# A decoder layer on one core: attention output at the next step's front, operands made in the preceding loops, ScalarE's and VectorE's heads written out

## The chip, the cores and the metric

The kernel runs on one core of one Trainium2 chip. The metric is the device time of one execution, in microseconds (us). Short names of the engines: PE is TensorE (matmuls), ACT is ScalarE, DVE is VectorE, POOL is GpSimd, SP is SyncE, which here issues nearly all transfers. SBUF holds operands, PSUM the products of PE.

## The reference

One inference step of one decoder layer over 520 columns: 512 prompt tokens and 8 sequences with one new token each (`D_MODEL` 2048, `D_FF` 5632, all f32).

```
h = rms_norm(x, norm_mix)
z = h @ w_in                       # q_a k_a v_a | q_r f_r i_r g_r, 8 + 8 heads of 128
...
o_att = rms_norm(o_att, att_gain) * (1.0 - lam_init)
...
o_rnn = rms_norm(o_rnn.astype(x.dtype), rnn_gain) * jax.nn.silu(g_r...)
x = x + jnp.concatenate([o_att, o_rnn], axis=-1) @ w_out
ffn, conv_buf = conv_ffn(rms_norm(x, norm_ffn), conv_buf0, w_gate, w_up, conv_w, conv_b, w_down)
x = x + ffn
x = x + jax.nn.sigmoid(rms_norm(x, norm_ple) @ w_ple_gate) * (p @ w_ple_proj)
```

`o_att` is differential attention (two softmaxes, the second subtracted with a weight), `o_rnn` a gated linear recurrence with a state. `conv_ffn` is silu(causal conv of 3 over h W_gate) times (h W_up), times W_down. Keys, values and states are outputs too.

## The kernel before

**Weights.** Every weight matrix comes in chunks of 8 tiles of 128x128 (6 and 5 in W_down). SP's `load` fetches a chunk into one of two raw buffers. ACT's `split` rounds it to `w_hi`, DVE's `low` makes the remainder `w_lo`. PE's `passes` then run five matmuls for each tile (lines 914 to 918) over the 520 columns of the activation, which is held in two parts too (`act_hi` and `act_lo`, both called act in the rows). A `split` waits until PE has used the chunk two before it (`w_used`). Products alternate between two PSUM banks, G[0] and G[1]. DVE empties a bank with `scaled` (lines 1467 to 1471) or `added` (lines 1475 and 1477, into the residual xT), which frees it for PE (`product_free`).

**Small products.** Everything else on PE is a small task in one of two scratch banks, M[0] and M[1], in turn. A task waits until the reader of the task two before it has set `free` of that bank.

**Heads.** There are 9 steps. Step h multiplies the 14 chunks of head h in the order q, k, v, f, i, r, g (28 slots of 4 tiles), with the attention of head h and the recurrence of head h − 1 as small tasks behind the slots that the tables `ATTENTION` and `RECURRENCE` name. The last step has only the recurrence and takes chunks of W_out. q uses bank 0, and so does g. PE's steps are written out; on ACT, DVE and SP the seven steps from 1 to 7 are a loop (`Fori`). At the front of a step PE runs a tiny product (`pad`, which ends the step before) and `ssq_a`, the sum of squares of the attention output; `att_out`, the attention output itself (weights wT times v_nat, 20 matmuls, line 797), stands behind slot 25 of its own step. From `ssq_a` ACT and DVE make the normalised output mix_a, which goes to memory; SP waits for it (`mix_a_done`) ahead of its loads of the key pages.

**Between the stages.** The next product's operands are made by ACT (`operand`, a copy scaled by the norm's gain) and DVE (the remainder, line 1712), k = 0 to 15, after the loop of the preceding stage, at both boundaries: W_out to ConvFFN, and ConvFFN to the last stage (PLE). Before the first ConvFFN product PE also sums the squares of x (`ss_out`, line 716), and ACT's `norm` makes the factor R from it: a table load, Ln, a table load, Exp. ConvFFN has 4 groups of 11 blocks; in the first block of each, PE runs `c_old` (line 1008) behind two chunks, a turn of old convolution rows that 11 transfers (`conv_in`) bring.

Of the kernel before, what the change touches and what calls it, by code (L numbers as in the profile page):

```python
# [65 lines left out]
KC = 8  # L66
# [34 lines left out]
}  # L101
RECURRENCE = {
    0: ["ssq_a"], 3: ["i_nat"], 7: ["kh_nat"], 9: ["upd"], 11: ["intra"], 14: ["rnn"], 16: ["s_upd"], 18: ["s_rnn"], 19: ["s_rnn_turn"], 20: ["ssq_r"],
# [72 lines left out]
EARLY_MIXED = 3  # L176
# [53 lines left out]
def program(nc, a, o):  # L230
# [56 lines left out]
    wT = hb("wT", [P, 10, P])  # L287
    k_pages = hb("k_pages", [P, NPG, P])
    k_nat = hb("k_nat", [P, 5, P])
    v_nat = hb("v_nat", [P, 5, P])  # L290
# [189 lines left out]
    def _(sp):  # L480
# [62 lines left out]
        def step(plan, it, h, r, pages):  # L543
            attention = any("ssq_q" in x for x in plan)
            recurrence = any("ssq_r" in x for x in plan)
            for s in range(HALVES):
                if attention and (not isinstance(h, int) or s >= 2 * EARLY_CHUNKS):
                    weights(h, s)
                if not attention and s % 2 == 0:
# [37 lines left out]
        def visit(what, arg):  # L587
# [4 lines left out]
            elif what == "heads":  # L592
# [3 lines left out]
                elif h1 == HEADS:  # L596
# [11 lines left out]
                    b, v = scratch.task("att_out", HEADS - 2)  # L608
# [4 lines left out]
                    for k in range(HEADS // 2, KT):  # L613
                        if k not in MIX_DIRECT:
                            mix_back(k)
                    for k in MIX_DIRECT:
                        x_back(k)
# [19 lines left out]
            elif what == "ffn":  # L637
                with sp.Fori(0, GROUPS) as g:
# [19 lines left out]
                    with sp.Fori(0, KT // 2) as m:  # L658
                        for j in range(4):
                            k0, n = ((0, 6), (6, 5))[j % 2]  # L660
                            load(g * GROUP_CHUNKS + m * 4 + (C_FFN + FF_CHUNKS + j), j % 2, w_down, g * GF + k0, n, m * (2 * P) + (j // 2) * P)
            elif what == "ple":
# [17 lines left out]
    def _(pe):  # L680
# [38 lines left out]
        def small(name, it, h, r):  # L719
# [73 lines left out]
            elif name == "att_out":  # L793
                b = task(name, it, [], (), ["w2", "w3", "v_nat"])
# [4 lines left out]
            elif name == "ssq_a":  # L799
                wide(name, it, [("sq_a", n)], K("ones"), sq)  # L800
# [53 lines left out]
        def step(plan, it, h, r):  # L854
            if r is not None:
                small("ssq_a", it, r, None)
            for s in range(HALVES):
# [25 lines left out]
                for name in plan[s]:  # L883
                    if name != "ssq_a":
                        small(name, it, h, r)
            pad(it)
# [34 lines left out]
        def full_product(g, n_free, c, sizes, x, wait_k=None, slot0=0, k0=0, wait_last=None):  # L921
# [3 lines left out]
            for j, n in enumerate(sizes):  # L925
# [6 lines left out]
                k += n  # L932

        sum_task = None

        def visit(what, arg):
# [33 lines left out]
            elif what == "out":  # L970
# [24 lines left out]
                wide("ss_out", 0, [("sq_sum_done", SUM_EARLY + KT)], K("ones"), sq_sum)  # L995
                pad(0)
            elif what == "ffn":
                with pe.Fori(0, GROUPS) as g:
                    def ff_block(f, first):
                        n = g * GF + f  # L1000
                        for x in range(2):
                            full_product(x, g * g_per_group + f + g_ffn[x], g * GROUP_CHUNKS + f * 4 + (C_FFN + 2 * x), (KC, KC), act2,
                                         ("act_lo_ready", 2 * KT + 1) if first and x == 0 else None)
# [14 lines left out]
                    with pe.Fori(0, KT // 2) as m:  # L1018
                        pe.wait_ge(flag("u_done"), g * GF + (GF - 1))
                        for x in range(2):  # L1020
                            full_product(x, g * g_per_group + m + (g_ffn[x] + GF), g * GROUP_CHUNKS + m * 4 + (C_FFN + FF_CHUNKS + 2 * x), DOWN_TILES, u2,
                                         wait_last=("u_done", g * GF + GF))
            elif what == "mid":
# [49 lines left out]
    def _(act):  # L1073
# [18 lines left out]
        def small(name, it, h, r):  # L1092
            n = None if h is None else h + 1
            m = None if r is None else r + 1
            if name in ("ssq_q", "ssq_k", "ssq_r"):
# [8 lines left out]
                elif name == "ssq_q":  # L1104
                    if h is not None and not isinstance(h, int):
# [10 lines left out]
            elif name in ("k_nat", "v_nat"):  # L1116
                dst, outs = (k_nat, ("k_prompt", "k_sample")) if name == "k_nat" else (v_nat, ("v_prompt", "v_sample"))
                b = take(name, it)
                if not isinstance(h, int):
# [35 lines left out]
            elif name == "att_out":  # L1155
# [3 lines left out]
                sb_, sv = scratch.task("s_turn", it)  # L1159
                act.wait_ge(free[sb_], sv)  # L1160
# [35 lines left out]
        def step(plan, it, h, r):  # L1196
            for s in range(HALVES):
# [22 lines left out]
                if r is not None and s == 0:  # L1220

# [8 lines left out]
                    func(r_e[:, :], r_k[:, 0:SEQ], ACT.Ln, bias=K("tiny")).then_inc(flag("log_k"), 1)  # L1230
                    b = take("ssq_a", it)
# [19 lines left out]
                for name in plan[s]:  # L1251
                    if name != "ssq_a":
# [15 lines left out]
        def operand(k, src, gain):  # L1268

            func(act_hi[:, k, :], src, ACT.Copy, scale=gain).then_inc(flag("act_hi_ready"), 1)  # L1270
# [22 lines left out]
        def visit(what, arg):  # L1293
# [30 lines left out]
            elif what == "heads":  # L1324
# [3 lines left out]
                elif h1 == HEADS:  # L1328
                    with act.Fori(h0, h1) as h:
# [3 lines left out]
            elif what == "out":  # L1333
# [17 lines left out]
                func(pT_hi[:, :, :], pT[:, :, :], ACT.Copy).then_inc(flag("pT_hi_done"), 1)  # L1351
                with act.Fori(KT // 4, KT // 2) as it:
                    for x in range(2):
                        out_product(it, x)
                for k in range(KT):
# [4 lines left out]
                    operand(k, xT[:, k, :], vec(ROWS_A["norm_ffn"] + k))  # L1360
                norm(*scratch.task("ss_out", 0))
            elif what == "ffn":
                with act.Fori(0, GROUPS) as g:
                    def ff_block(f, first):
# [7 lines left out]
                        if first:  # L1372
                            b = take("c_old", g)
# [18 lines left out]
                    with act.Fori(0, KT // 2) as m:  # L1392
                        for x in range(2):
# [3 lines left out]
                            squares(g * KT + m * 2 + (SUM_EARLY + KT + x), x, column(xT, m * 2 + x))  # L1397
            elif what == "mid":
                for k in range(KT):
                    act.wait_ge(w_used, C_PLE)  # L1400
                    if k >= KT - 2:
                        act.wait_ge(g_free[k % 2], g_ple[k % 2])
                    operand(k, xT[:, k, :], vec(ROWS_A["norm_ple"] + k))
# [46 lines left out]
    def _(dve):  # L1450
# [34 lines left out]
        def small(name, it, h, r):  # L1485
# [34 lines left out]
            elif name.startswith("score"):  # L1520
# [4 lines left out]
                if i > 0 or not isinstance(h, int):  # L1525
# [95 lines left out]
        def step(plan, it, h, r):  # L1621
            for s in range(HALVES):
# [60 lines left out]
                if r is not None and s == 6:  # L1683
                    dve.wait_ge(flag("exp_b"), r + 1)
                    dve.wait_ge(flag("r_qm_done"), r + 1)
                    dve.tensor_tensor(r_qd, z_r[:, 0:SEQ], r_e[:, :], ALU.mult).then_inc(flag("r_qd_done"), 1)
                if h is not None and s in ROTATE_AT:
# [4 lines left out]
            pad(it)  # L1692
# [16 lines left out]
        def operand(k, src, gain, n):  # L1709

            dve.wait_ge(flag("act_hi_ready"), n)
            dve.scalar_tensor_tensor(act_lo[:, k, :], src, gain, act_hi[:, k, :].bitcast(F32), ALU.mult, ALU.subtract).then_inc(flag("act_lo_ready"), 1)  # L1712
# [17 lines left out]
        def visit(what, arg):  # L1730
# [54 lines left out]
            elif what == "heads":  # L1785
# [3 lines left out]
                elif h1 == HEADS:  # L1789
                    with dve.Fori(h0, h1) as h:  # L1790
# [3 lines left out]
            elif what == "out":  # L1794
# [17 lines left out]
                with dve.Fori(KT // 4, KT // 2) as it:  # L1812
                    for x in range(2):
                        out_product(it, x)
                pad(0)
                for k in range(KT):
                    operand(k, xT[:, k, :], vec(ROWS_A["norm_ffn"] + k), 2 * KT + k + 1)
                dve.wait_ge(flag("R_ready"), 2)
            elif what == "ffn":
# [3 lines left out]
                with dve.Fori(0, GROUPS) as g:  # L1823
                    with dve.Fori(0, GF) as f:
# [14 lines left out]
                        dve.wait_ge(full[b], v - 1)  # L1839
                        scaled(0, ffg[:, 2:T + 2], g * g_per_group + f + (g_ffn[0] + 1))  # L1840
# [20 lines left out]
                        dve.tensor_tensor(column(u_lo, f), ffu[:, :], column(u_hi, f).bitcast(F32), ALU.subtract).then_inc(flag("u_done"), 1)  # L1861
                    dve.memset(sq_sum[:, :], 0.0).then_inc(flag("sum_zeroed"), 1)
                    with dve.Fori(0, KT // 2) as m:
                        for x in range(2):
# [7 lines left out]
                            add_squares(g * KT + m * 2 + (SUM_EARLY + KT + x), x)  # L1872
            elif what == "mid":
                pad(0)
                for k in range(KT):
                    operand(k, xT[:, k, :], vec(ROWS_A["norm_ple"] + k), 3 * KT + k + 1)
# [100 lines left out]
```

## Time and profile before

| | before |
|---|---|
| time, median of 3 runs | 2856.32 us (2855.97 to 2856.54) |
| the profiled execution's own time | 2855.82 us |
| its span in the profile | 2854.0 us |
| PE busy | 2807.3 us (98%) |
| DVE busy | 1514.7 us (53%) |
| ACT busy | 1042.5 us (37%) |
| mean granted clock of PE | 0.993 |

PE, a matmul pipeline whose ends are modelled, is hardly ever idle over the whole span. A granted clock of 1.00 is the higher of its two levels (2.4 GHz), 0.50 the lower (1.2 GHz).

### The profile page before, as it was taken

To read this page: it belongs to the slowest core of one execution; us is meant where nothing else is said; L and a number is where in the kernel's file an instruction comes from. 1 tells how busy PE (TensorE), PEld (TensorE's weight loads), DVE (VectorE), ACT (ScalarE), POOL (GpSimd) and SP (SyncE) were. 2 spreads that over 40 slices of the span, in tenths; PEclk is the share of its full clock that TensorE was granted. 3 is DMA by queue.
4 is the path that set the end of the run, shared out by engine and by line. 5 is a ranking of instruction groups with operands and counts; after the bars stand their busy time and mean duration, and the time that the engine had idled before them with its cause. 6 is when DMAs were issued, how large, how long until landed. Compare 5 with 4: busy or idle time off the path is not lost.

```text
span 2854.0 us, 53939 instructions
## 1 busy us (share of the span) xinstructions
PE 2807.3 (98%) x20395; PEld 2583.9 (91%) x20395; DVE 1514.7 (53%) x2547; ACT 1042.5 (37%) x1457; POOL 20.1 (1%) x19
## 2 busy tenths in 40 slices
PE   6999999999999999999999999999999999999998
PEld 6888888888888998999999999999999999998998
DVE  5565565565566545445544445544455444455444
ACT  4455455455455234222332223322223322234322
POOL 2000000000000000000000000000000000000000
PEclk8999999999999999999999999999999999999999
DMA  5343343343345332332333332333323333332332
GB/s 195 99 124 105 101 123 109 96 124 111 97 125 189 111 89 82 88 95 82 92 100 88 90 94 84 93 97 88 91 84 94 97 91 88 89 88 85 106 110 83
DMA packets 547886, 291.20 MB, mean 102 GB/s; under 512 B 15848, under 2 KB 538914, under 8 KB 547786
## 3 DMA queue, kind: packets, MB, share of 16 engines
q1 hardware_dynamic: 516762, 268.49, 32.4%
q10 hardware_dynamic: 31040, 21.46, 2.4%
q8 instruction: 69, 1.13, 0.2%
q14 instruction: 15, 0.12, 0.0%
HBM read 268.44 MB, written 21.63 MB: 102 GB/s over the span
## 4 chain that ended last, share of the span: by engine, by line
PE 93%; DVE 4%; ACT 1%; issue 1%; ACTq 0%; SPq 0%; DVEq 0%; DMA 0%
PE product L914 28%; PE product L918 15%; PE product L916 15%; PE product L915 14%; PE product L917 14%; PE scratch L708 2%; PE scratch L716 1%; DVE w_lo L1454 1%; DVE act L1712 1%; PE scratch L797 1%; PE scratch L758 1%; DVE s_state L1607 1%; ACT w_hi L1079 1%; ACT score L1090 0%; PE scratch L813 0%
## 5 line engine op out<-in xcount | busy, mean ns | idle before, releaser
L914 PE MATMUL product<-act,w_hi 128*128 128x512 f32 x2816 | 1142.3, 406 | 21.1 <-DVE act L1712 14.2
L1454 DVE TENSOR_TENSOR w_lo<-w_raw,w_hi 128x1024 fp32r<-128x1024 f32 (+1 forms) x496 | 594.4, 1198 | 562.2 <-ACT w_hi L1079 561.9
L1079 ACT ACTIVATE w_hi<-w_raw 128x1024 fp32r<-128x1024 f32 (+1 forms) x496 | 514.7, 1038 | 975.7 <-PE product L918 941.2
L918 PE MATMUL product<-act,w_lo 128*128 128x264 f32 x2816 | 806.4, 286 | 0.0
L916 PE MATMUL product<-act,w_hi 128*128 128x264 f32 x2816 | 802.2, 285 | 0.0
L915 PE MATMUL product<-act,w_hi 128*128 128x264 f32 x2816 | 800.6, 284 | 0.0
L917 PE MATMUL product<-act,w_lo 128*128 128x256 f32 x2816 | 793.2, 282 | 0.0
L916 PEld LDWEIGHTS product<-act,w_hi 128*128 128x128 f32 x2816 | 531.3, 189 | 128.2
L914 PEld LDWEIGHTS product<-act,w_hi 128*128 128x128 f32 x2816 | 534.3, 190 | 46.7 <-issue 38.9
L915 PEld LDWEIGHTS product<-act,w_hi 128*128 128x128 f32 x2816 | 533.9, 190 | 0.8
L918 PEld LDWEIGHTS product<-act,w_lo 128*128 128x128 f32 x2816 | 533.4, 189 | 0.0
L917 PEld LDWEIGHTS product<-act,w_lo 128*128 128x128 f32 x2816 | 531.1, 189 | 0.0
L914 PE MATMUL product<-u,w_hi 128*128 128x512 f32 x704 | 278.5, 396 | 0.0
L1467 DVE TENSOR_TENSOR low_part<-product,R 128x256 f32<-128x256 f32 x160 | 67.6, 423 | 292.0 <-PE product L918 289.3
L916 PE MATMUL product<-u,w_hi 128*128 128x264 f32 x704 | 200.1, 284 | 0.0
L915 PE MATMUL product<-u,w_hi 128*128 128x264 f32 x704 | 199.3, 283 | 0.0
L918 PE MATMUL product<-u,w_lo 128*128 128x264 f32 x704 | 198.8, 282 | 0.0
L917 PE MATMUL product<-u,w_lo 128*128 128x256 f32 x704 | 197.0, 280 | 0.0
L916 PEld LDWEIGHTS product<-u,w_hi 128*128 128x128 f32 x704 | 132.1, 188 | 31.5
L1475 DVE TENSOR_TENSOR xT<-product,xT 128x520 f32 (+1 forms) x96 | 67.1, 699 | 160.2 <-PE product L918 160.2
L914 PEld LDWEIGHTS product<-u,w_hi 128*128 128x128 f32 x704 | 132.1, 188 | 0.8 <-DVE w_lo L1454 0.7
L918 PEld LDWEIGHTS product<-u,w_lo 128*128 128x128 f32 x704 | 132.7, 188 | 0.0
(251 smaller groups left out, 2266.4 us busy)
## 6 DMA issues: line engine op xcount, KB each, us to landing
w_raw<-in_w_in SPq DMA_DIRECT2D x112, 512.0 KB, 3.8
w_raw<-in_w_gate SPq DMA_DIRECT2D x88, 512.0 KB, 3.8
w_raw<-in_w_up SPq DMA_DIRECT2D x88, 512.0 KB, 3.8
w_raw<-in_w_down SPq DMA_DIRECT2D x64, 384.0 KB, 3.3
w_raw<-in_w_down SPq DMA_DIRECT2D x64, 320.0 KB, 3.1
w_raw<-in_w_out SPq DMA_DIRECT2D x32, 512.0 KB, 4.1
w_raw<-in_w_ple_gate SPq DMA_DIRECT2D x32, 384.0 KB, 3.3
k_pages<-in_cache_k SPq DMA_DIRECT2D x128, 64.0 KB, 2.5
```

Source lines behind the costliest of these rows:

```text
L708: return pe.transpose(out, in_, ident[0:n, 0:n])
L716: mm = pe.matmul(M[b][:, half, 0:TH], lhsT, rhs[:, half * TH:(half + 1) * TH], start=True, stop=True)
L758: mm = pe.matmul(M[b][:, m_, 0:w], q_rot[rows, i * P:(i + 1) * P], k_rot[rows, 0:w], start=True, stop=True)
L914: pe.matmul(both, hi, x[:, k, :, 0:TA], start=begin, stop=False)
L915: pe.matmul(far, hi, x[:, k, 1, TA:T], start=begin, stop=False)
L916: pe.matmul(far, hi, x[:, k, 0, TA:T], start=False, stop=False)
L917: pe.matmul(near, lo, x[:, k, 1, 0:TA], start=False, stop=end)
L918: mm = pe.matmul(far, lo, x[:, k, 1, TA:T], start=False, stop=end)
L1079: act.activation(w_hi[:, slot, 0:n, :], w_raw[:, slot, 0:n, :], ACT.Copy).then_inc(w_hi_ready, 1)
L1454: dve.tensor_tensor(flat(w_lo[:, slot, 0:n, :]), flat(w_raw[:, slot, 0:n, :]), flat(w_hi[:, slot, 0:n, :]).bitcast(F32), ALU.subtract).the ...
L1467: dve.tensor_tensor(low_part[:, :], low_sums(G[g]), R[:, 0:TA], ALU.mult).then_inc(g_low[g], 1)
L1475: dve.tensor_tensor(x, high_sums(G[g]), x, ALU.add).then_inc(g_low[g], 1)
```

## The change

- `att_out` moves from behind slot 25 of its step to the front of the next, and `ssq_a` from the front to behind slot 1. `pad` moves from the end of a step to behind slot 26. On ACT the copy of `att_out` and the Square that feeds `ssq_a` move with it, and so does the read of `ssq_a`. In the last step SP fetches most parts of the mixed output after `s_turn`, a task before `att_out`, and the rest after `att_out`; four, not three, of DVE's early mixes come first.
- ACT's and DVE's loops over the heads become written-out code.
- The ConvFFN operands 0 to 7 are made inside the second half of the W_out loop, 8 to 15 after it. `ss_out` runs behind the first ConvFFN chunk, and ACT's `norm` behind the splits of two chunks.
- All PLE operands are made inside the down loop of the last group. For that, group 0 on every engine and the last group on ACT and DVE are written apart.
- SP issues a group's 11 `conv_in` transfers ahead of its first two chunks, not behind them.

```diff
-    21: ["score3"], 22: ["w2"], 24: ["w3", "s_out"], 25: ["s_turn", "att_out"],
+    21: ["score3"], 22: ["w2"], 24: ["w3", "s_out"], 25: ["s_turn"],
...
-    0: ["ssq_a"], 3: ["i_nat"], 7: ["kh_nat"], ...
+    0: ["att_out"], 1: ["ssq_a"], 3: ["i_nat"], 7: ["kh_nat"], ...
...
-EARLY_MIXED = 3
+EARLY_MIXED = 4
+PAD_AT = 26
...
             if r is not None:
-                small("ssq_a", it, r, None)
+                small("att_out", it, r, None)
...
-            pad(it)
+                if s == PAD_AT:
+                    pad(it)
...
-                wide("ss_out", 0, [("sq_sum_done", SUM_EARLY + KT)], K("ones"), sq_sum)
+                sum_task = scratch.task("ss_out", 0)
...
+                def sum_out():
+                    sum_of_squares(SUM_EARLY + KT)
...
+                                         after=sum_out if isinstance(g, int) and first and x == 0 else None)
...
                 if r is not None and s == 0:
+                    small("att_out", it, r, None)
...
+                if r is not None and s == 1:
                     b = take("ssq_a", it)
...
-                    with act.Fori(h0, h1) as h:
+                    for h in range(h0, h1):
                         step(plan, h - 1, h, h - 1)
...
+                act.wait_ge(w_used, C_RNN)
                 with act.Fori(KT // 4, KT // 2) as it:
                     for x in range(2):
                         out_product(it, x)
-                for k in range(KT):
+                        operand_of("norm_ffn", it * 2 + (x - KC))
+                for k in range(KC, KT):
...
-                norm(*scratch.task("ss_out", 0))
+                norm_task = scratch.task("ss_out", 0)
...
                         two_chunks(0)
                         if first:
+                            if isinstance(g, int) and g == 0:
+                                norm(*norm_task)
                             b = take("c_old", g)
...
+                            if final:
+                                operand_of("norm_ple", m * 2 + x)
...
-                    with dve.Fori(h0, h1) as h:
+                    for h in range(h0, h1):
...
-                    ffn_chunk(0, 0)
-                    ffn_chunk(0, 1)
-
-                    sp.wait_ge(full[0], scratch.task("c_old", g)[1] - 1)
-
-                    sp.wait_ge(flag("conv_out"), g * 32 + 16)
+                    if isinstance(g, int):
+                        sp.wait_ge(flag("pT_lo_done"), 1)
+                    else:
+                        sp.wait_ge(full[0], scratch.task("c_old", g)[1] - 1)
...
                         sp.dma_start(conv_in[j:j + 2 * NS, i // 2, :], ...).then_inc(flag("conv_in"), 16)
+                    ffn_chunk(0, 0)
+                    ffn_chunk(0, 1)
```

How PE's order changes between the first two steps. Before, behind the last tile of the g product (its last matmul is the first row):

```order
L918 MATMUL product<-act,w_lo 128x264
L852 MATMUL scratch<-const 32x64 [waits scratch1_free]
L716 MATMUL scratch<-sqx,const 128x260 [waits sq_a,scratch0_free]
L716 MATMUL scratch<-sqx,const 128x260
L914 MATMUL product<-act,w_hi 128x512 [waits product0_free,w_lo_ready]
```

And of the change, the same place, and behind the eight tiles of slots 0 and 1 (the program lines of `passes` are now 926 to 930):

```order
L930 MATMUL product<-act,w_lo 128x264
L808 MATMUL scratch<-wT,v_nat 128x128 [waits scratch0_free]
L808 MATMUL scratch<-wT,v_nat 128x128 x9
L926 MATMUL product<-act,w_hi 128x512 [waits product0_free,w_lo_ready]
...
L930 MATMUL product<-act,w_lo 128x264
L727 MATMUL scratch<-sqx,const 128x260 [waits sq_a,scratch1_free]
L727 MATMUL scratch<-sqx,const 128x260
L926 MATMUL product<-act,w_hi 128x512 [waits w_lo_ready]
```

Ten products (`att_out`; the profile counts each as two matmuls) stand where the pad and `ssq_a` stood, and `ssq_a` has moved eight tiles on.

How ACT's order changes between W_out and ConvFFN. Before, with act an operand, R the norm's factor, product0 and product1 the two product banks:

```order
L1090 ACTIVATE act<-xT,vecs 128x520 [waits w_used] x14
L1090 ACTIVATE act<-xT,vecs 128x520 [waits product0_free,w_used]
L1090 ACTIVATE act<-xT,vecs 128x520 [waits product1_free,w_used]
L1090 ACT_TABLE_LOAD
L1090 ACTIVATE R<-scratch,const 128x520 [waits scratch0_full]
L1090 ACT_TABLE_LOAD
L1090 ACTIVATE R<-R 128x520 [waits scratch0_free]
...
L1079 ACTIVATE w_hi<-w_raw 128x1024 [waits w_used]
...
L1090 ACTIVATE conv_old<-scratch 128x2x6x16 [waits scratch0_full]
```

And of the change:

```order
L1112 ACTIVATE act<-xT,vecs 128x520 [waits w_used] x6
L1112 ACTIVATE act<-xT,vecs 128x520 [waits product0_free,w_used]
L1112 ACTIVATE act<-xT,vecs 128x520 [waits product1_free,w_used]
L1101 ACTIVATE w_hi<-w_raw 128x1024 [waits w_used,w_landed0]
L1101 ACTIVATE w_hi<-w_raw 128x1024 [waits w_used,w_landed1]
L1112 ACT_TABLE_LOAD
L1112 ACTIVATE R<-scratch,const 128x520 [waits scratch0_full]
L1112 ACT_TABLE_LOAD
L1112 ACTIVATE R<-R 128x520 [waits scratch0_free]
L1112 ACTIVATE conv_old<-scratch 128x2x6x16 [waits scratch0_full]
```

Eight operands are gone from here, and the two splits now stand ahead of the two operations on R. On PE the tasks of that place, before `c_old` and after it in the change (line 1026), read:

```order
L727 MATMUL scratch<-sq_sum,const 128x260 [waits sq_sum_done,scratch0_free]
L727 MATMUL scratch<-sq_sum,const 128x260
L926 MATMUL product<-act,w_hi 128x512 [waits act_lo_ready,w_lo_ready]
...
L1026 MATMUL scratch<-const,conv_in 128x16 [waits conv_in,scratch0_free]
L1026 MATMUL scratch<-const,conv_in 128x16 x10
L926 MATMUL product<-act,w_hi 128x512 [waits w_lo_ready,product1_free]
```

`ss_out` now stands between the first and the second chunk, and `c_old`, behind the second, uses the same scratch bank.

## Rows read from the trace of the kernel before

**Rows 1.** The page, busy time, share of the span and instructions of PE:

```profile
PE 2807.3 (98%) x20395; PEld 2583.9 (91%) x20395; DVE 1514.7 (53%) x2547; ACT 1042.5 (37%) x1457; POOL 20.1 (1%) x19
```

**Rows 2.** Waits of PE: total us, times, longest us.

```profile
PE product L914 <- DVE act L1712: 14.2, 8, 4.3
...
PE product L914 <- DVE z_g L1468: 6.8, 8, 2.2
...
PE scratch L843 <- DVE s_ro L1613: 1.4, 7, 0.2
```

**Rows 3.** Timeline of PE around a step's front: start us, us, instruction, [idle before].

```profile
244.52 2.48 PE L797 MATMUL scratch<-wT,v_nat 128*128 128x128 f32 x20
...
252.89 1.14 PE L716 MATMUL scratch<-sqx,const 128*128 128x260 f32 x4
254.79 0.47 PE L914 MATMUL product<-act,w_hi 128*128 128x512 f32 x1 [0.76 <-DVE z_g L1468]
...
255.59 0.40 PE L914 MATMUL product<-act,w_hi 128*128 128x512 f32 x1
...
276.11 1.04 PE L716 MATMUL scratch<-sqx,tables 128*128 128x260 f32 x4
...
277.69 0.39 PE L914 MATMUL product<-act,w_hi 128*128 128x512 f32 x1
...
278.41 0.40 PE L914 MATMUL product<-act,w_hi 128*128 128x512 f32 x1
...
280.21 0.47 PE L914 MATMUL product<-act,w_hi 128*128 128x512 f32 x1
```

**Rows 4.** Timeline of PE, front of the last step:

```profile
894.58 0.47 PE L914 MATMUL product<-act,w_hi 128*128 128x512 f32 x1 [2.18 <-DVE z_g L1468]
```

**Rows 5.** Timeline of DVE around the same step's front:

```profile
253.61 0.42 DVE L1467 TENSOR_TENSOR low_part<-product,R 128x256 f32<-128x256 f32 x1 [0.47 <-issue]
...
275.02 1.23 DVE L1454 TENSOR_TENSOR w_lo<-w_raw,w_hi 128x1024 fp32r<-128x1024 f32 x1 [3.79 <-ACT w_hi L1079]
```

**Rows 6.** Timeline of ACT around the same step's front:

```profile
247.04 0.60 ACT L1090 ACTIVATE oT<-scratch 128x512 f32<-128x512 f32 x1 [2.16 <-PE scratch L797]
...
253.84 1.28 ACT L1090 ACT_TABLE_LOAD   x1
...
273.93 1.06 ACT L1079 ACTIVATE w_hi<-w_raw 128x1024 fp32r<-128x1024 f32 x1 [2.07 <-DMA w_raw<-in_w_in]
```

**Rows 7.** Timeline of PE, W_out to ConvFFN:

```profile
1092.18 2.07 PE L716 MATMUL scratch<-sq_sum,const 128*128 128x260 f32 x4 [3.29 <-DVE sq_sum L1719]
...
1108.70 1.51 PE L1008 MATMUL scratch<-const,conv_in 16*128 16x16 f32 x22
```

**Rows 8.** Timeline of ACT there:

```profile
1102.36 0.70 ACT L1090 ACTIVATE R<-scratch,const 128x520 f32<-128x520 f32 x1
```

**Rows 9.** Windows: length, busy PE, PEld, DVE, ACT, POOL; granted clock, DMA share, GB/s.

```profile
892.00:898.00 6.00, 3.82 (x26) 3.23 (x24) 5.90 (x12) 5.59 (x7) 0.00 (x0) 1.00 1.06 368
1092.00:1098.80 6.80, 5.62 (x18) 4.30 (x19) 4.19 (x9) 6.80 (x12) 0.00 (x0) 0.50 0.04 10
2626.00:2634.00 8.00, 7.26 (x37) 6.74 (x38) 8.00 (x13) 8.00 (x14) 0.00 (x0) 0.79 0.17 49
```

**Rows 10.** Timeline of PE, ConvFFN to PLE:

```profile
2626.74 0.47 PE L914 MATMUL product<-act,w_hi 128*128 128x512 f32 x1 [3.70 <-DVE act L1712]
```

**Rows 11.** Timeline of SP's queue, group 0 to 1; the page's DMA issues (KB, us to landing).

```profile
1457.94 8.15 SPq L495 DMA_DIRECT2D w_raw<-in_w_down  x3
1469.88 4.04 SPq L495 DMA_DIRECT2D w_raw<-in_w_gate  x2
1474.17 5.55 SPq L652 DMA_DIRECT2D conv_in<-in_state_ffn_conv  x11
...
w_raw<-in_w_gate SPq DMA_DIRECT2D x88, 512.0 KB, 3.8
```

**Rows 12.** Timeline of ACT, group 0 to 1:

```profile
1475.16 1.06 ACT L1079 ACTIVATE w_hi<-w_raw 128x1024 fp32r<-128x1024 f32 x1 [2.07 <-PE product L918]
```

More of the change, by code:

```diff
@@ L548, in step @@
                     weights(h, s)
+                if not attention and s == 0:
+                    b, v = scratch.task("att_out", it)
+                    sp.wait_ge(full[b], v)
+                    for k in range(MIX_DIRECT[0] + 1, MIX_DIRECT[1]):
+                        mix_back(k)
+                    x_back(MIX_DIRECT[1])
                 if not attention and s % 2 == 0:
@@ L607, in visit @@
                         mix_back(k)
-                    b, v = scratch.task("att_out", HEADS - 2)
+                    b, v = scratch.task("s_turn", HEADS - 2)
                     sp.wait_ge(full[b], v)
@@ L612, in visit @@
                     sp.wait_ge(flag("v_nat_out"), HEADS * 32)
[L613 to L617, printed above, removed]
+                    for k in range(HEADS // 2, MIX_DIRECT[0]):
+                        mix_back(k)
+                    x_back(MIX_DIRECT[0])
                 else:
@@ L637, in visit, with group @@
             elif what == "ffn":
-                with sp.Fori(0, GROUPS) as g:
+                def group(g):
                     def ffn_chunk(f, j):
@@ L661, in visit @@
                             load(g * GROUP_CHUNKS + m * 4 + (C_FFN + FF_CHUNKS + j), j % 2, w_down, g * GF + k0, n, m * (2 * P) + (j // 2) * P)
+                group(0)
+                with sp.Fori(1, GROUPS) as g:
+                    group(g)
             elif what == "ple":
@@ L932, in full_product @@
                 k += n
+                if after is not None and j == 0:
+                    after()
         sum_task = None
@@ L1022, in visit @@
                                          wait_last=("u_done", g * GF + GF))
+                group(0)
+                with pe.Fori(1, GROUPS) as g:
+                    group(g)
             elif what == "mid":
@@ L1158, in small @@
                 act.wait_ge(free[b], scratch.task(name, it)[1])
-                sb_, sv = scratch.task("s_turn", it)
-                act.wait_ge(free[sb_], sv)
+                sb_, sv = scratch.task("ssq_a", it)
+                act.wait_ge(free[sb_], sv - 1)
                 func(sq[:, :], oT[:, :], ACT.Square).then_inc(flag("sq_a"), 1)
@@ L1251, in step @@
                 for name in plan[s]:
-                    if name != "ssq_a":
+                    if name not in ("ssq_a", "att_out"):
                         small(name, it, h, r)
@@ L1397, in visit @@
                             squares(g * KT + m * 2 + (SUM_EARLY + KT + x), x, column(xT, m * 2 + x))
-            elif what == "mid":
[L1399 to L1403, printed above, removed]
+                            if final:
+                                operand_of("norm_ple", m * 2 + x)
+                group(0)
+                with act.Fori(1, GROUPS - 1) as g:
+                    group(g)
+                group(GROUPS - 1, final=True)
+            elif what == "mid":
                 norm_task = scratch.task("ss_ffn", 0)
@@ L1691, in step @@
                         small(name, it, h, r)
-            pad(it)
             if r is not None and h is not None:
@@ L1872, in visit @@
                             add_squares(g * KT + m * 2 + (SUM_EARLY + KT + x), x)
+                            if final:
+                                operand_of("norm_ple", m * 2 + x, m * 2 + (3 * KT + x + 1))
+                ff_block(0, 0)
+                with dve.Fori(1, GF) as f:
+                    ff_block(0, f)
+                down(0)
+                with dve.Fori(1, GROUPS - 1) as g:
+                    with dve.Fori(0, GF) as f:
+                        ff_block(g, f)
+                    down(g)
+                with dve.Fori(0, GF) as f:
+                    ff_block(GROUPS - 1, f)
+                down(GROUPS - 1, final=True)
             elif what == "mid":
                 pad(0)
-                for k in range(KT):
-                    operand(k, xT[:, k, :], vec(ROWS_A["norm_ple"] + k), 3 * KT + k + 1)
             elif what == "ple":
```

48 lines of the change are left out of this document (28 added, 20 removed).

## The prediction

> **What bounds the kernel now.** I read the page first: TensorE (PE) is busy 98% of a span of 2854.0 us, so only what PE waits for, and what a slow clock costs it, can be won [rows 1]. Next the waits of PE. Three entries belong to places that the change touches: 14.2 us for act (the operands of a matrix product), 6.8 us in 8 pieces for z_g and 1.4 us for s_ro [rows 2]. Of act's only what the timeline shows at the two stage boundaries below can be won; the setup and the last stage are left alone. Then I opened the timeline at each place to see what a wait costs with its restart.
>
> **Front of a head's step (att_out and ssq_a).** The last product of a step lies in bank 0, and the first of the next step needs that bank. Between them PE has a tiny pad and ssq_a, and then waits for VectorE's z_g. From ssq_a's start to the second tile pass 255.59 − 252.89 = 2.70 us; the same four matmuls in mid-stream take 277.69 − 276.11 = 1.58 us [rows 3]. The boundary costs 1.12 us, of which 0.76 is printed as idle; 0.36 is restart. Eight boundaries: 6.8 + 8 × 0.36 = 9.7 us.
> The change puts att_out there instead. Its 20 matmuls take 2.48 us to their last end [rows 3], and they need nothing of the step's last product. VectorE needs 254.79 − 253.61 = 1.18 us from low_part's start to z_g's release, and began 0.47 us late behind "issue", the loop's back-edge [rows 3, 5]; even 0.47 + 1.18 = 1.65 us fits under 2.48. ssq_a then runs between two slots, where it costs its mid-stream price, 1.58 − 0.72 = 0.86 us (a tile is 278.41 − 277.69 = 0.72) [rows 3]; it loses nothing but its place. The work itself is the same. At the last boundary VectorE does early mixes ahead of z_g and PE idles 2.18 us [rows 4]; now four of them, but with the pad's wait gone they can begin before the step's last product ends, so I leave 0.3 us. Term: **9.4 us** (6.0 if the restarts stay and 0.8 us is left at the last boundary; 9.7 at most).
>
> *What becomes late.* ScalarE's copy of att_out (0.60 us) and a Square as long stood far ahead of the boundary, at 247.04; now they stand behind att_out. That would start near 252.7 and end near 255.2, so copy and Square last to 256.4 and the table load that was at 253.84 follows then: **2.5 us later** [rows 3, 6]. Behind it queue the gates of the recurrence, the rsqrt of ssq_a, and by it mix_a; SP holds k_pages, and with them weight loads, until mix_a is done. The split at 273.93 shows this: it waited 2.07 us for its weights. Its w_lo is done at 275.02 + 1.23 = 276.25 and PE comes to that chunk at 280.21: 3.96 us of slack [rows 3, 5, 6]. 2.5 us of it go, nothing is paid. This is cover that a slower transfer would use up (rival C).
>
> **Heads of ScalarE and VectorE without loops.** One row shows a loop's price: "issue" 0.47 us ahead of low_part, already counted above [rows 5]. Elsewhere the only tight wait is s_ro, 1.4 us in seven steps [rows 2]; constants in place of registers may shorten its chain by some of that. No row says how much: 0 to 1.4, and I take the middle, **0.7 us**.
> The Trainium skill, "Runtime: NRT & Kernel Launch" (Instruction fetch mechanics), says that fetch is sequential and mostly hidden, and that a taken branch out of the fetched window stalls. The 0.47 us, once in each turn of the loop, agrees with the second half; by that alone the loops would give back at most 6 × 0.47 = 2.8 us, and here those lie under att_out in any case. No row shows the first half for VectorE.
>
> **Output projection to ConvFFN.** Before: PE's last tile ends at 1092.18 − 3.29 = 1088.89, it waits 3.29 us for sq_sum, runs the sum of squares at half clock, waits again for act, and reaches c_old at 1108.70, two weight chunks later [rows 2, 7]. After: operands 0 to 7 were made in the loop, so the first chunk starts near 1089.05 behind the pad; 8 tiles × 0.72 bring 1094.8; the sum of squares 0.86 brings 1095.65; the second chunk ends at 1101.4. Operands 8 to 15 begin as soon as the loop ends, and the whole first chunk, 5.75 us, lies ahead of the tile that needs the first of them.
> Here a **new wait** comes. c_old and ss_out share scratch bank 0, so c_old must wait until ScalarE's Ln has read the sum. The change puts that Ln behind the split of the chunk after next, which may begin only when PE has finished the chunk just before c_old. So from 1101.4: split 1.06, table load 1.28, Ln 0.70 and some 0.2 us of hand-overs, 3.2 us [rows 6, 8]. c_old starts at about 1104.7: 4.0 us earlier than before, not the 7.2 us that the chunks had won.
> PE idles 3.2 us there, and what followed such pauses differs: after 3.29 us the granted clock was 0.50 for 6.8 us; after 2.18 us it stayed 1.00; after 3.70 us it was 0.79 over 8 us [rows 4, 7, 9, 10]. That is a loss of 0, of 8 × 0.21 = 1.7, or of up to half of 5.62 busy us, 2.8. I take 1.7. Term: **2.3 us** (1.2 to 4.0).
>
> **ConvFFN to PLE.** All 16 operands now come out of the last down loop. PE waited 3.70 us for them and then ran 8 us at a clock of 0.79: 3.70 + 1.7 = **5.4 us** [rows 9, 10]; at least 3.7, if a wait for a scratch bank stops the clock from staying up. The scratch bank of the sum of squares is not needed again until a chunk later; ScalarE's Ln, no longer behind 16 operands, is in time.
>
> **conv_in ahead of a group's first chunks.** SP's 11 issues take 5.55 us and now stand before w_gate's two. SP is free from 1457.94 + 8.15 = 1466.1, so w_gate goes out near 1472.0, not at 1469.88; it lands 3.8 us later (the median of its 88), at 1475.8. The split took it at 1475.16, having waited for PE, so it comes 0.7 us later; split, w_lo and hand-over (1.06 + 1.23 + 0.2) bring 1478.3, and PE needs it 5 tiles after 1475.1, at 1478.7 [rows 11, 12]. Hidden by 0.4 us. With the spread of landings I charge **0.4 us** for three boundaries; 3 us if each is 1 us late.
>
> **Sum.** 9.4 + 0.7 + 2.3 + 5.4 − 0.4 = 17.4 us. The profiled execution took 2855.82 us itself, 0.5 under the median of 2856.32; from the median the forecast is 2838.9, so **2839 us**. Bounds: least 6.0 + 0 + 1.2 + 3.7 − 3 = 7.9 (2848.4), most 9.7 + 1.4 + 4.0 + 5.4 = 20.5 (2835.8).
>
> **Rivals.**
> A. *No stop at c_old.* If the Ln reads its sum before that split, both chunks' gain stays: 7.2 and no clock loss instead of 2.3, so 2834. Against it speaks the program order on ScalarE, which puts both splits first; for it only that a hand-over could be missing from my reading.
> B. *The heads' wait moves.* If z_g is late from another cause (the mixes, or a low_part that queues behind a late w_lo), the heads give only the back-edges, 2.8 us, instead of 10.1: 17.4 − 7.3 = 10.1, so 2846. VectorE is busy half of the time, and z_g has 0.8 us to spare under att_out; little speaks for this.
> C. *Slower: the heads' weights come late.* ScalarE's chain is 2.5 us later in each of seven steps, and SP's page loads and weight loads with it. It costs nothing up to 3.96 us. If queueing on SP doubles the delay to 5.0, PE waits 1.0 us a step; that makes 7 us and still a gain. Slower than now it would be from 17.4 / 7 = 2.5 us a step on, a delay of 6.5 us; at 7 us, 3.0 × 7 = 21, so 2860. The rows show only 2.07 us of waiting for a transfer there, so I give it little.
> D. *Nothing to measure.* Were C's delay some 5.5 to 7 us, or the written-out code slow to arrive by as much, gain and loss would cancel: 2852 to 2860. PE's heads are written out already, and PE waits for nothing but other engines.
>
> **Chances.** My forecast, all terms within their bounds, 0.74 (2835 to 2844); A 0.10; B 0.09; C 0.04; D 0.03. The range 2834 to 2846 takes in A and B's edge. Some 0.2% (5.7 us) is what a measurement here can tell from no change: faster 0.92, within 0.2% 0.04, slower 0.04.
>
> **What would show it.** In the profile after, z_g should be gone from PE's waits, and the step of a head be some 1.1 us shorter. A wait of PE's c_old line for ScalarE's R of about 3.2 us, with a granted clock under 1 behind it, would show the new stop; if it is absent, A holds. At the start of PLE no wait for act and a full clock. At the three group boundaries no wait for w_lo. A wait of PE for w_lo in mid-step, or for z_g still, would prove the head term wrong.

## The result, and the profile after

The changed kernel takes 2840.29 us (median of 6 runs, 2838.44 to 2841.87), the kernel before 2856.14 us beside it (6 runs, 2855.35 to 2856.69): 15.85 us less, a ratio of 0.9944 with a 95% interval of 0.9931 to 0.9957. The profiled execution took 2838.44 us, the shortest of the six; its span is 2836.7 us.

The page, as [rows 1], and waits of PE, as [rows 2] (total us, times, longest us):

```profile
PE 2799.5 (99%) x20395; PEld 2580.4 (91%) x20395; DVE 1516.2 (53%) x2547; ACT 1034.1 (36%) x1450; POOL 20.0 (1%) x19
```

```profile
PE product L926 <- DVE act L1747: 9.6, 7, 4.3
...
PE scratch L727 <- DVE sq_sum L1758: 3.3, 1, 3.3
PE scratch L1026 <- ACT R L1112: 3.2, 1, 3.2
...
PE scratch L727 <- ACT sqx L1112: 1.0, 1, 1.0
PE product L926 <- DVE w_lo L1488: 0.7, 2, 0.4
...
PE scratch L854 <- DVE s_ro L1647: 0.2, 1, 0.2
```

z_g (6.8 us before) is gone, and act has fallen from 14.2 to 9.6 us. What is left of act, the 3.3 us for sq_sum and the 1.0 us for sqx lie in the setup. The fall of s_ro from 1.4 to 0.2 looks larger than it is: the list leaves out waits below 0.15 us, and in PE's timeline each of the seven has only shrunk from some 0.19 to 0.14 us. Two entries behind the setup are new: c_old (line 1026) waits 3.2 us for R, and PE twice for w_lo.

Both kernels run the same 3520 weight tiles in the same order, so the starts of the same tile in both timelines say where time was won. The last column is the change of the difference since the row above.

| a tile just behind | before, us | after, us | difference | won here |
|---|---|---|---|---|
| the setup | 72.21 | 70.75 | 1.46 | 1.46 |
| front of step 1 | 154.90 | 152.43 | 2.47 | 1.01 |
| front of step 2 | 261.32 | 257.72 | 3.60 | 1.13 |
| front of step 7 | 793.26 | 784.18 | 9.08 | 5.48 |
| front of the last step | 901.11 | 889.49 | 11.62 | 2.54 |
| the last step's small tasks | 980.91 | 969.60 | 11.31 | −0.31 |
| c_old of group 0, and the slow clock behind it | 1112.40 | 1098.74 | 13.66 | 2.35 |
| start of group 1 | 1479.27 | 1465.82 | 13.45 | −0.21 |
| start of group 2 | 1859.91 | 1847.04 | 12.87 | −0.58 |
| start of group 3 | 2241.27 | 2229.01 | 12.26 | −0.61 |
| start of PLE (its sixth tile) | 2631.94 | 2614.55 | 17.39 | 5.13 |

The −0.31 us in the last step is the pad, which now stands behind slot 26 there.

The 1.46 us in the setup are not the change's: up to that tile PE, ACT and DVE run the same instructions in both. The clock differed. From 60 to 68 us the granted clock was 0.57 before and 1.00 after (windows as [rows 9], before and after):

```profile
60.00:68.00 8.00, 5.90 (x20) 5.25 (x21) 3.33 (x15) 4.71 (x8) 0.47 (x2) 0.57 0.45 125
```

```profile
60.00:68.00 8.00, 5.83 (x38) 5.43 (x39) 4.18 (x20) 4.78 (x8) 0.47 (x2) 1.00 0.42 119
```

Five of the seven other profiled executions below that have the changed kernel's setup reach the same tile 0.8 to 1.4 us later, with a granted clock of 0.57 to 0.79 there; the other two have 1.00 and reach it at the same time. Without the setup 15.9 us are left, which is what the medians differ by.

A step's front after, as [rows 3]; PE's timeline, start us, us, instruction:

```profile
248.17 2.39 PE L808 MATMUL scratch<-wT,v_nat 128*128 128x128 f32 x20
250.32 0.48 PE L926 MATMUL product<-act,w_hi 128*128 128x512 f32 x1
...
256.14 1.04 PE L727 MATMUL scratch<-sqx,const 128*128 128x260 f32 x4
256.82 0.58 PE L926 MATMUL product<-act,w_hi 128*128 128x512 f32 x1
...
276.63 0.47 PE L926 MATMUL product<-act,w_hi 128*128 128x512 f32 x1
```

att_out runs 2.39 us and the first tile follows with no idle time printed. On DVE and ACT, as [rows 5, 6]:

```profile
248.47 0.43 DVE L1501 TENSOR_TENSOR low_part<-product,R 128x256 f32<-128x256 f32 x1 [3.02 <-PE product L930]
248.81 0.69 DVE L1502 TENSOR_TENSOR z_g<-product,R 128x520 f32<-128x520 f32 x1
...
272.26 1.23 DVE L1488 TENSOR_TENSOR w_lo<-w_raw,w_hi 128x1024 fp32r<-128x1024 f32 x1 [4.61 <-ACT w_hi L1101]
```

```profile
250.60 0.60 ACT L1112 ACTIVATE oT<-scratch 128x512 f32<-128x512 f32 x1 [1.09 <-PE scratch L808]
251.23 0.64 ACT L1112 ACTIVATE sqx<-oT 128x520 f32<-128x520 f32 x1
251.89 1.28 ACT L1112 ACT_TABLE_LOAD   x1
...
271.17 1.06 ACT L1101 ACTIVATE w_hi<-w_raw 128x1024 fp32r<-128x1024 f32 x1 [2.88 <-DMA w_raw<-in_w_in]
```

z_g is ready at 249.5, 0.8 us before PE asks for its bank at 250.32. ACT's table load comes 251.89 − 248.17 = 3.72 us after the step's front; before, 253.84 stood 0.95 us behind ssq_a's start at 252.89, with the pad ahead of that. Counted from the end of the step's last product, the chain is thus about 2.5 us later, as worked out ahead. PE itself comes 0.9 us later to the chunks behind slot 1, since ssq_a now runs ahead of them. Against PE's tiles, which are 3.60 us earlier here, the table load is therefore only 1.65 us later (253.84 − 3.60 = 250.24, now 251.89), the page loads in SP's queue 1.3 us (266.17 − 3.60 = 262.57, now 263.86), and the weight split behind them 0.8 us (273.93 − 3.60 = 270.33, now 271.17). Its w_lo is done at 273.49, 3.1 us before PE's tile at 276.63.

That is one chunk. Two chunks earlier, the cover from the end of w_lo to PE's tile went from 4.3 us to 3.0, before and after:

```profile
261.89 1.23 DVE L1454 TENSOR_TENSOR w_lo<-w_raw,w_hi 128x1024 fp32r<-128x1024 f32 x1 [0.26 <-ACT w_hi L1079]
...
267.40 0.50 PE L914 MATMUL product<-act,w_hi 128*128 128x512 f32 x1
```

```profile
259.58 1.22 DVE L1488 TENSOR_TENSOR w_lo<-w_raw,w_hi 128x1024 fp32r<-128x1024 f32 x1
...
263.81 0.50 PE L926 MATMUL product<-act,w_hi 128*128 128x512 f32 x1
```

Of the chunks that lost cover, one in the last step has the least left. At that step's third chunk it went from 1.4 us (w_lo done at 905.80, the tile at 907.21) to 0.4:

```profile
893.93 1.22 DVE L1488 TENSOR_TENSOR w_lo<-w_raw,w_hi 128x1024 fp32r<-128x1024 f32 x1
...
895.58 0.50 PE L926 MATMUL product<-act,w_hi 128*128 128x512 f32 x1
```

W_out to ConvFFN, PE as [rows 7], and ACT as [rows 8]:

```profile
1083.55 1.04 PE L727 MATMUL scratch<-sq_sum,const 128*128 128x260 f32 x4
...
1093.53 1.51 PE L1026 MATMUL scratch<-const,conv_in 16*128 16x16 f32 x22 [3.21 <-ACT R L1112]
1094.97 0.79 PE L926 MATMUL product<-act,w_hi 128*128 128x512 f32 x1
...
1096.43 0.63 PE L926 MATMUL product<-act,w_hi 128*128 128x512 f32 x1
```

```profile
1090.42 1.06 ACT L1101 ACTIVATE w_hi<-w_raw 128x1024 fp32r<-128x1024 f32 x1 [4.08 <-PE product L930]
1091.49 1.28 ACT L1112 ACT_TABLE_LOAD   x1
1092.79 0.69 ACT L1112 ACTIVATE R<-scratch,const 128x520 f32<-128x520 f32 x1
```

The split ends ACT's wait when PE ends the chunk; table load and Ln follow, and c_old starts 0.05 us after Ln. The tiles behind it stand 1.46, 1.30 and 1.01 us apart instead of 0.72; from 1095.0 to 1098.4 the granted clock was 0.50.

At PLE's start there is no wait, tiles follow at 0.72 us from the first, and the granted clock of the 8 us is 1.00 [rows 9, 10]:

```profile
2610.00:2618.00 8.00, 8.00 (x54) 7.20 (x54) 4.64 (x7) 4.77 (x6) 0.00 (x0) 1.00 0.34 100
```

At a group's start ACT now waits for w_gate, at the same places as [rows 11, 12] (SP's queue at groups 1 and 2, ACT at group 1, PE at groups 2 and 3):

```profile
1452.93 5.36 SPq L656 DMA_DIRECT2D conv_in<-in_state_ffn_conv  x11
1458.54 1.78 SPq L497 DMA_DIRECT2D w_raw<-in_w_gate  x2
...
1840.54 1.36 SPq L497 DMA_DIRECT2D w_raw<-in_w_gate  x2
```

```profile
1462.62 1.06 ACT L1101 ACTIVATE w_hi<-w_raw 128x1024 fp32r<-128x1024 f32 x1 [3.21 <-DMA w_raw<-in_w_gate]
```

```profile
1847.04 0.50 PE L926 MATMUL product<-act,w_hi 128*128 128x512 f32 x1 [0.38 <-DVE w_lo L1488]
...
2229.01 0.50 PE L926 MATMUL product<-act,w_hi 128*128 128x512 f32 x1 [0.34 <-DVE w_lo L1488]
```

### The profile page after: what moved, and what is told of

The parts are those of the page before. It is cut to its first block, busy times and chain, and to the rows that moved or that the text cites. A ratio compares the mean times of both kernels' runs of the same rounds, so it can differ in the third digit from the quotient of the medians.

```text
span 2836.7 us, 53314 instructions
## 1 busy us (share of the span) xinstructions
PE 2799.5 (99%) x20395; PEld 2580.4 (91%) x20395; DVE 1516.2 (53%) x2547; ACT 1034.1 (36%) x1450; POOL 20.0 (1%) x19
## 4 chain that ended last, share of the span: by engine, by line
PE 93%; DVE 3%; ACT 2%; issue 1%; SPq 1%; DMA 0%; ACTq 0%; DVEq 0%
PE product L926 28%; PE product L930 14%; PE product L928 14%; PE product L927 14%; PE product L929 14%; PE scratch L719 2%; PE scratch L727 1%; DVE w_lo L1488 1%; ACT w_hi L1101 1%; ACT score L1112 1%; PE scratch L808 1%; DVE act L1747 1%; PE scratch L769 1%; DVE s_state L1641 1%; PE scratch L824 0%
```

## The experiments

Theory: att_out covers z_g at the steps' fronts whatever the loops cost; both stage boundaries win by operands made earlier; c_old's new wait comes from Ln's place behind a split; conv_in's place costs a little. The rivals are named in each expectation. The first four kernels shared their runs of the kernel before (median 2857.03 us), the last four too (2856.67 us).

**Is it the moved att_out or the written-out code?** The changed kernel with loops again:

```diff
-                    for h in range(h0, h1):
+                    with act.Fori(h0, h1) as h:
...
-                    for h in range(h0, h1):
+                    with dve.Fori(h0, h1) as h:
```

> The changed kernel with the heads of ScalarE and VectorE in loops again, all else as changed. Theory 1 (att_out at the front covers z_g whatever the loop costs): the back-edge of 0.47 us and the 1.18 us to z_g fit under att_out, PE has no wait for z_g at the steps' fronts, only the waits for s_ro come back: 0.9 to 1.4 us more than the changed kernel, some 2841.5 us. Theory 2 (the loop's back-edge was the wait, and the written-out code won the heads' time): PE waits for z_g again in six steps, 0.47 to 0.76 us each with 0.36 us of restart: 5 to 7 us more, some 2846 us.

Measured: 2841.12 us, 0.9944 of before (0.9931 to 0.9958). PE's waits:

```profile
PE scratch L854 <- DVE s_ro L1647: 1.9, 7, 0.3
```

No entry for z_g. s_ro's waits are 0.27 us or a little more, longer than in the kernel before. Against the changed kernel its tiles fall back by some 0.14 us in each of the seven steps, at s_ro: from 0.83 us behind at the end of the setup to 1.83 us behind at the end of the heads, 1.0 us. The medians, each against its own runs of before, do not tell these 1.0 us (15.9 us gained by both); 5 to 7 us they would have told. Theory 1.

The other way round, the kernel before with only its heads written out:

> The kernel before with the heads of ScalarE and VectorE written out and nothing else of the change. Theory 1: the wait for z_g shrinks by the back-edge, 6 x 0.47 = 2.8 us, and s_ro gives 0.9 us; 0.3 us of idle and the restarts stay at six fronts and the last front keeps its 2.18 us: some 2852.4 us. Theory 2 (written-out code wins the heads' time): all of the heads' 9.9 us but the last front's 2.5: some 2849 us.

Measured: 2852.88 us, 0.9985 (0.9976 to 0.9994).

```profile
PE product L914 <- DVE z_g L1468: 3.7, 8, 2.0
```

z_g fell from 6.8 to 3.7 us, by 3.1; at the front of step 2 the "issue" of 0.47 us ahead of low_part is gone. s_ro's waits are below the list's 0.15 us. By the tiles the heads are 4.1 us shorter (0.22 us ahead of the kernel before at the end of the setup, 4.36 at the last step's front). Loops were worth some 4 us, but three of these lie where att_out covers them anyway. Theory 1.

**Why c_old waits.** The changed kernel with `norm` between the two splits:

```diff
                             for j in (2 * x + 2, 2 * x + 3):
+                                if j == 3 and first and isinstance(g, int) and g == 0:
+                                    norm(*norm_task)
                                 split(...)
                         two_chunks(0)
                         if first:
-                            if isinstance(g, int) and g == 0:
-                                norm(*norm_task)
```

> The changed kernel with ScalarE's two operations on R (Ln and Exp of the sum of squares) between the two splits of the first ConvFFN block instead of behind both. Theory 1 (c_old waits for Ln because Ln stands behind a split that waits for the chunk just before c_old): the wait of 3.2 us and the half clock behind it, 1.5 us, go: 4.7 us less than the changed kernel, some 2835.6 us, and the granted clock stays 1.00 there. Theory 2 (the stop only moves: the second split comes later by Ln, Exp and two table loads, and PE waits for the next chunk's w_lo or for R instead): less than 1.5 us gained, a new wait at the same place.

Measured: 2835.27 us, 0.9924 (0.9910 to 0.9937). PE, and ACT:

```profile
1090.22 1.51 PE L1026 MATMUL scratch<-const,conv_in 16*128 16x16 f32 x22
1091.66 0.50 PE L926 MATMUL product<-act,w_hi 128*128 128x512 f32 x1
...
1092.47 0.39 PE L926 MATMUL product<-act,w_hi 128*128 128x512 f32 x1
```

```profile
1086.33 1.28 ACT L1112 ACT_TABLE_LOAD   x1
1087.62 0.70 ACT L1112 ACTIVATE R<-scratch,const 128x520 f32<-128x520 f32 x1
1088.34 1.28 ACT L1112 ACT_TABLE_LOAD   x1
1089.63 0.64 ACT L1112 ACTIVATE R<-R 128x520 f32<-128x520 f32 x1
1090.39 1.06 ACT L1101 ACTIVATE w_hi<-w_raw 128x1024 fp32r<-128x1024 f32 x1
```

All four operations on R fit into the time in which ACT had waited for PE, and the split comes when it did before. The tile table against the changed kernel gains 3.3 us at c_old and 4.8 us three tiles on, the rest being the clock, which stayed at 1.00 here. Theory 1.

**conv_in.** The changed kernel with a group's two first weight chunks ahead of conv_in again:

```diff
+                    ffn_chunk(0, 0)
+                    ffn_chunk(0, 1)
                     if isinstance(g, int):
...
-                    ffn_chunk(0, 0)
-                    ffn_chunk(0, 1)
                     ffn_chunk(0, 2)
```

> The changed kernel with a group's conv_in transfers issued behind its first two weight chunks again, as before the change. Theory 1 (the eleven issues delay w_gate, and w_lo comes late at three group boundaries): PE's waits for w_lo of 0.7 us go and with the restarts 1.4 us are won: some 2838.9 us. Theory 2 (the waits are an accident of landings, or the conv_in then come too late for c_old): no change or slower, 2840.3 us or more.

Measured: 2839.43 us, 0.9938 (0.9924 to 0.9951), 17.6 us under its runs of before, where the changed kernel is 15.9 under its own; a difference less than these intervals tell apart. The timelines tell it: against the changed kernel the tiles gain 0.17, 0.56 and 0.61 us at the starts of groups 1 to 3, 1.3 us together, and no wait for w_lo is left. Theory 1, by the profile. This run shows another thing: c_old after the same pause of 3.21 us took 2.73 us, not 1.51, so here the half clock began at once (granted 0.50 over all of it).

```profile
1094.75 2.73 PE L1026 MATMUL scratch<-const,conv_in 16*128 16x16 f32 x22 [3.21 <-ACT R L1112]
```

**How much cover is left in a step.** The changed kernel with more copies in ACT's chain behind the Square (the kernel with 3; the other has 8):

```diff
-                func(sq[:, :], oT[:, :], ACT.Square).then_inc(flag("sq_a"), 1)
+                func(sq[:, :], oT[:, :], ACT.Square).then_inc(flag("late"), 1)
+                for i in range(3):
+                    act.wait_ge(flag("late"), h * 3 + i + 1)
+                    func(sq[:, :], sq[:, :], ACT.Copy).then_inc(flag("sq_a" if i == 2 else "late"), 1)
```

> The changed kernel with three more copies (0.64 us each, some 2.0 us together) in ScalarE's queue behind the Square of the attention output, so that its chain at each step's front is later by that. Theory 1 (the front's chain has cover: in the changed kernel w_lo is done 3.0 us before PE comes to its chunk, at two places of a step): no cost, 2840 us give or take 1.5. Theory 2 (ScalarE's chain is on the path of the step): 2.0 us in each of eight fronts, some 2856 us.

Measured: 2840.53 us, 0.9947 (0.9932 to 0.9962). The time is the same, and up to the last step's front nothing is lost, as theory 1 has it: the tiles are 0.81 us behind the changed kernel's at the end of the setup and 0.91 us there. But at the third chunk of the last step, which had 0.4 us of cover left, PE now waits for w_lo:

```profile
897.56 0.50 PE L926 MATMUL product<-act,w_hi 128*128 128x512 f32 x1 [1.00 <-DVE w_lo L1491]
```

The tiles fall from 0.91 to 1.97 us behind. The medians are too coarse to tell this 1 us. Theory 1 holds for seven fronts of eight.

> The same with eight copies, some 5.4 us. Theory 1: 5.4 - 3.0 = 2.4 us late and 0.36 us of restart in each of eight fronts, some 22 us more than the changed kernel: 2862 us, with PE waiting for w_lo in mid-step. If the weight loads behind the page loads slip by less than the chain, as the changed kernel's do (0.8 us for 2.4), then half of it. Theory 2: 5.4 us in each front, 43 us, some 2883 us.

Measured: 2863.47 us, 1.0023 (1.0014 to 1.0032), 23 us more than the changed kernel. PE's waits from 140 to 885 us, in seven steps:

```profile
PE product L926 <- DVE w_lo L1491: 7.6, 8, 1.0
PE scratch L727 <- ACT sqx L1112: 7.5, 7, 1.1
```

The size was right and its making only half: PE waits 1.0 us a step for w_lo, and as long for sqx, the Square itself, which ssq_a needs two slots into the step. In the changed kernel sqx is ready at 251.87 and wanted at 256.14, 4.3 us of cover, of which 5.4 us of copies leave none. In the last step PE waits 2.3 us for sqx. Between 2.0 and 5.4 us of delay the cover of the seven steps ends; that of the last step ends below 2.0. That is rival C, forced: late enough, the change would lose.

**The operands of PLE.** The changed kernel with the operands made after the last down loop:

```diff
-                            if final:
-                                operand_of("norm_ple", m * 2 + x)
...
+                for k in range(KT):
+                    act.wait_ge(w_used, C_PLE)
+                    if k >= KT - 2:
+                        act.wait_ge(g_free[k % 2], g_ple[k % 2])
+                    operand(k, xT[:, k, :], vec(ROWS_A["norm_ple"] + k))
```

(and the same on DVE).

> The changed kernel with the sixteen operands of the last stage made after the last down loop again. The term of 5.3 us comes back as a whole if it is a matter of its own: some 2845.6 us, with a wait of 3.7 us for act and a granted clock near 0.8 behind it. Rival: a part of it was won by the groups written apart or by ScalarE's earlier Ln, then less comes back, under 3.5 us.

Measured: 2846.15 us, 0.9966 (0.9953 to 0.9979), 10.5 us under its runs of before: 5.3 of the changed kernel's 15.9 us are gone.

```profile
2614.80 0.76 PE L926 MATMUL product<-act,w_hi 128*128 128x512 f32 x1 [3.70 <-DVE act L1750]
...
2616.24 0.63 PE L926 MATMUL product<-act,w_hi 128*128 128x512 f32 x1
```

The wait is 3.70 us again. Its slow clock cost more than before the change, since it began with the first tile (1.44 us to the second; before the change 0.80): over 8 us the granted clock was 0.58, not the 0.8 that was expected. The term is a matter of its own.

**Both repairs together.** `norm` between the splits, and conv_in behind w_gate:

> The changed kernel with ScalarE's Ln and Exp between the two splits and conv_in behind the first two weight chunks of a group. The two gains touch different places and should add: 4.8 + 1.3 = 6.1 us less than the changed kernel, some 2834.2 us; PE's waits for R and for w_lo both gone. If late conv_in now hold up c_old, which comes 3.2 us earlier in group 0, a new wait of c_old for a transfer appears and the gain is under 5 us.

Measured: 2833.11 us, 0.9919 (0.9906 to 0.9933), the fastest kernel here. PE waits neither for R nor for w_lo, and c_old waits for nothing. Its tiles gain 4.7 us on the changed kernel at c_old (from 0.82 behind to 3.88 ahead) and 1.4 us over the group starts, 6.1 together. Against its own runs of before it wins 23.6 us, 7.7 more than the change; the single repairs, reckoned in the same way, win 5.9 (2857.03 − 2835.27 − 15.85) and 1.7 (2857.03 − 2839.43 − 15.85). They add.

## Why the prediction was right

2839 us were forecast, 2840.29 measured; of 17.4 us, 15.9 came. Step by step:

- **Front of the steps, 9.4 + 0.7 us:** 1.01 + 1.13 + 5.48 + 2.54 − 0.31 = 9.85 us measured. The mechanism held: att_out covers z_g with 0.8 us to spare, and the restart of 0.36 us goes with the wait. The written-out code gives 0.07 us at s_ro and 0.09 us at slot 25 in each of seven steps, as it also does in the kernel before with only its heads written out: some 1.1 us in place of 0.7, and only the smaller part of it where it was sought. The front itself is left with some 8.7 us of the 9.4. One cost was not in the sum: the pad, 0.23 us ahead of ssq_a in the front before (252.66 to 252.89), costs 0.4 us in mid-step (0.31 us at its own tile in the last step, 0.10 us at the next).
- **What becomes late:** from the step's front the chain is 2.5 us later, as worked out; that 2.5 us of the 3.96 us of cover would go was wrong. Only 0.8 us went at that chunk. The working set the whole delay against the slack and left out that PE comes 0.9 us later too, behind ssq_a; of the rest, 1.65 us, 1.3 us reached the page loads and 0.8 us the split. Nor was 3.96 us the cover of every chunk: it was 1.4 us in the last step, where 0.4 us are left. That nothing is paid came out right with little to spare there. Three copies more cost 1 us in the last step and nothing before it, eight cost 23 us.
- **W_out to ConvFFN, 2.3 us:** 2.35 measured, and by the mechanism named: a new wait of c_old for ACT's Ln, forecast at 3.2 us and measured at 3.21. Moving Ln alone takes it away: that kernel's tiles are 11.34 us ahead of the kernel before at the last step's small tasks and 18.48 us behind c_old, so it wins 7.1 us at this boundary, near the 7.2 us that the chunks were said to win.
- **ConvFFN to PLE, 5.4 us:** 5.13 measured in the profiled execution, 5.3 by undoing it.
- **conv_in, −0.4 us:** 1.4 us were lost (0.21 + 0.58 + 0.61). This term was mis-sized. The forecast worked out group 1 alone, took the median landing of w_gate, 3.8 us, let the split start with it, and found 0.4 us to spare. At the group starts w_gate lands 3.9 to 4.0 us after its issue, before the change and after it, so the eleven transfers ahead did not slow it; the split starts 0.1 to 0.2 us after the landing (1462.62 − 1458.54 = 4.1 us in all). That uses up group 1's spare, and no wait is printed there. At groups 2 and 3 w_gate also goes out later against PE: 5.24 us before the start of the last down tile at group 2 (1845.78 − 1840.54), 5.70 at group 1 (1464.24 − 1458.54). So w_lo came late by 0.3 to 0.4 us there, with some 0.2 us of restart each. The bound of 3 us held, but the sign that was named, no wait for w_lo at the group boundaries, did not come.

Rival A (no stop at c_old) did not occur, but its time, 2834, is what the kernel with Ln moved reaches within 1.3 us. Rival B did not occur: z_g is gone even with the loops. C and D did not, since the delay stays inside the cover, by 0.4 us in the last step; the three copies there, and the eight copies in every step, show that C's mechanism exists.

The chance of 0.74 was given for 2835 to 2844, while the terms' own bounds add up to 2835.8 to 2848.4. The measured time lies in both.

What stays open: when the slow clock of a given execution starts, and so about 1 us of every median here; and whether the last step's third chunk lost its 1.0 us of cover to ACT's later chain or to SP's new order of transfers there.

## What to carry to other kernels

A wait at a loop's front is best filled with work that needs nothing of the last product: here 2.4 us of matmuls that stood elsewhere took away some 9 us of waits and restarts, and it mattered little whether the waiting engine itself became faster. When a reduction moves behind a product so that the product starts earlier, look who frees its bank next: the reader on the other engine moved too, behind an instruction that waits for that very product, and 4.8 of 7.1 us were lost until its place was changed. Read the cover that a delayed chain uses up at every chunk behind it: where one chunk had 3.1 us left, another had 0.4. Allow for a pause on TensorE twice, once as idle time and once for the slow tiles that may follow it.

## What the runs showed of the hardware

The same pause of PE costs differently from one execution to the next. After 3.21 us without a matmul, the granted clock fell to 0.50 behind c_old (1.51 us for its 22 matmuls in the changed kernel), before it (2.73 us in the kernel with conv_in behind) or during it (2.03 us in the kernel with eight copies). After 3.70 us at PLE's start the second tile came 0.80 us behind the first in the kernel before, and 1.44 us in the kernel with the operands made late. By the tiles behind these places, that moves a run by 1.0 to 1.5 us.

The clock need not fall at all. In the setup of the profiled execution of the changed kernel PE waited 3.27 us for sq_sum, and the granted clock of the 5.8 us behind it was 1.00; it was also 1.00 after the 2.18 us at the last step's front before the change, but 0.50 after 2.33 us in the last step with eight copies. The setup shows the price: the three profiled executions with 1.00 from 60 to 68 us are 0.8 to 1.4 us ahead of the five others of the same setup. These three lie 1.3 to 1.9 us below the medians of their own kernels, the five between 0.6 us below and 0.9 us above.
